# A ring of four weight buffers for both expert matmuls of a hybrid encoder block, with VectorE's work spread over a written-out loop

## What is computed

```python
q = (xt @ wq).reshape(T, PEER_HEADS, 2, PEER_HALF)
v1, i1 = lax.top_k(s1, PEER_TOPK)              # s1, s2: q against two sets of 128 keys
v2, i2 = lax.top_k(s2, PEER_TOPK)
best, flat = lax.top_k(cand, PEER_TOPK)        # cand: the 16 x 16 sums of v1 and v2
experts = e1 * N_KEYS + e2
gates = jax.nn.softmax(best, axis=-1)
a = jnp.einsum("td,thkd->thk", xb, u[eb])      # eb: 8 heads x 16 experts of a token
act = gb * jax.nn.gelu(a)
y = jnp.einsum("thk,thkd->td", act, v[eb])
```

## Time and profile before

| what | value |
|---|---|
| device time, median of 3 runs | 3211.02 us (3209.46 to 3213.96) |
| the profiled execution, first to last instruction | 3210.7 us |
| PE busy | 3014.2 us (94%) |
| DVE busy | 2610.3 us (81%) |
| ACT busy | 1091.2 us (34%) |
| POOL busy | 825.0 us (26%) |
| first to last v job's start | 2181.9 to 3205.9 us |
| first to last gelu of a u job | 1088.5 to 2181.5 us |

### The profile page before, as it was taken

One profiled execution on the slowest core, in us unless ns is written; L12 is line 12 of the kernel. 1 busy time (PEld: TensorE's weight loads), 2 busy tenths in 40 slices (PEclk: granted clock), 3 DMA queues, 4 the chain that ended last, 5 costly groups with the idle time before them and its releaser, 6 DMA issues.

```text
span 3210.7 us, 44193 instructions
## 1 busy us (share of the span) xinstructions
PE 3014.2 (94%) x17373; PEld 2771.7 (86%) x17373; DVE 2610.3 (81%) x3085; ACT 1091.2 (34%) x1132; POOL 825.0 (26%) x380
## 2 busy tenths in 40 slices
PE   4899989989899989999999999997899999999999
PEld 2687766557678989999989999987899999999999
DVE  6986868766763599999879999875798898988985
ACT  3322243431122334444323333322333333333331
POOL 4600000000020012333102322332354544444440
PEclk8999989999999999999999999998999999999999
DMA  8621224257644358778648999998899999999994
GB/s 359 262 99 71 72 86 154 103 217 299 256 170 158 142 191 297 295 290 299 250 177 340 356 365 367 367 372 336 342 379 392 391 385 389 383 388 394 384 389 158
DMA packets 182046, 892.83 MB, mean 278 GB/s; under 512 B 15664, under 2 KB 77232, under 8 KB 85808
## 3 DMA queue, kind: packets, MB, share of 16 engines
q1 hardware_dynamic: 111376, 491.29, 40.8%
q0 software_dynamic: 46080, 335.56, 26.6%
q10 hardware_dynamic: 24480, 64.45, 5.1%
HBM read 836.71 MB, written 54.53 MB: 278 GB/s over the span
## 4 chain that ended last, share of the span: by engine, by line
PE 73%; DVE 14%; DMA 6%; ACT 3%; issue 3%; POOL 1%; SPq 0%; DVEq 0%; ACTq 0%; PEldq 0%
PE bank L1592 11%; PE bank L1593 11%; PE bank L1594 11%; PE bank L1951 8%; PE bank L1953 8%; PE bank L1952 8%; PE bank L1925 2%; DVE w_lo L905 2%; DVE ada_w L930 2%; PE bank L1829 2%; PE bank L1830 2%; PE bank L1831 2%; DMA ada_w<-wada 1%; DMA u_row<-u_rows,urow_i 1%; PE bank L1634 1%
## 5 line engine op out<-in xcount | busy, mean ns | idle before, releaser
L1592 PE MATMUL bank<-act_hi,w_hi 128*128 128x352 f32 (+1 forms) x2584 | 886.7, 343 | 42.6 <-DVE w_lo L905 32.0
L1593 PE MATMUL bank<-act_lo,w_hi 128*128 128x352 f32 (+1 forms) x2584 | 879.5, 340 | 0.0
L1594 PE MATMUL bank<-act_hi,w_lo 128*128 128x352 f32 (+1 forms) x2584 | 876.9, 339 | 0.0
L1951 PE MATMUL bank<-wt_hi,w_hi 128*128 128x352 f32 x2048 | 666.2, 325 | 34.0 <-ACT stage L854 14.6
L905 DVE TENSOR_TENSOR w_lo<-w_raw,w_hi 128x2048 fp32r<-128x2048 f32 (+1 forms) x191 | 434.7, 2276 | 282.1 <-ACT w_hi L472 269.1
L1952 PE MATMUL bank<-wt_lo,w_hi 128*128 128x352 f32 x2048 | 662.5, 323 | 0.0
L1953 PE MATMUL bank<-wt_hi,w_lo 128*128 128x352 f32 x2048 | 662.4, 323 | 0.0
L472 ACT ACTIVATE w_hi<-w_raw 128x2048 fp32r<-128x2048 f32 (+1 forms) x199 | 375.6, 1887 | 810.2 <-PE bank L1594 547.5
L1592 PEld LDWEIGHTS bank<-act_hi,w_hi 128*128 128x128 f32 x2584 | 491.7, 190 | 71.3 <-issue 26.9
L1594 PEld LDWEIGHTS bank<-act_hi,w_lo 128*128 128x128 f32 x2584 | 493.4, 191 | 22.3
L1593 PEld LDWEIGHTS bank<-act_lo,w_hi 128*128 128x128 f32 x2584 | 492.3, 191 | 20.8 <-issue 0.2
(11 more groups left out here) (297 smaller groups left out, 3801.0 us busy)
## 6 DMA issues: line engine op xcount, KB each, us to landing
w_raw<-u SPq DMA_DIRECT2D x128, 1024.0 KB, 8.1
w_raw<-v SPq DMA_DIRECT2D x86, 1024.0 KB, 9.3
ada_w<-wada SPq DMA_DIRECT2D x80, 1024.0 KB, 5.8
v_raw<-v SPq DMA_DIRECT2D x42, 1024.0 KB, 9.3
w_raw<-win SPq DMA_DIRECT2D x27, 1024.0 KB, 4.8
gelu_scratch<-gelu_s ACTq DMA_DIRECT2D x128, 176.0 KB, 3.6
gate_scratch<-g_chunk ACTq DMA_DIRECT2D x11, 2048.0 KB, 14.3
wt<-gelu_scratch SPq DMA_DIRECT2D x32, 704.0 KB, 5.5
```

The source lines that it names most:

```text
L1592: pe.matmul(out, wh, hi_t(k), start=(k == 0), stop=False)
L1593: pe.matmul(out, wh, lo_t(k), start=False, stop=False)
L1594: last = pe.matmul(out, wl, hi_t(k), start=False, stop=(k == nk - 1))
L1951: pe.matmul(o, w_hi[s][:, col], th, start=begin is not None and e == 0, stop=False)
```

## The change

One ring of four buffers takes the raw weights of u and v jobs alike. The low half is written over the raw weight it was made of, so raw and low share a buffer, and three buffers hold high halves. The load of job g now waits until PE has finished job g-4, `hi` until PE has finished g-3. The u jobs are written out on all engines, and what DVE does between them is dealt out anew: selections write their results in place, 7 dots in 6 jobs instead of 6 in 6, three jobs for each block of indices instead of four, four more rows of `u` are gathered before the switch. The hot steps run with jobs 74 to 117 instead of 72 to 115. ACT does the gelu of a job before the high half of the job three ahead. The end of a segment no longer waits for PE's own last matmul.

```diff
+XU = 12
+SEL_G, TAB_G, SEL, TAB, HOT = 2, 10, 13, 61, 74
+N_HOTS = TD // 8
...
-        v_raw = [w_raw[J_V % 2], w_raw[1 - J_V % 2], at("v_raw2", 54, [P, CH])]
+        raw = [w_raw[1], w_raw[0], at("raw2", 104, [P, CH]), at("raw3", 96, [P, CH])]
+        low = [at("low0", 72, [P, CH], F32R), at("low1", 64, [P, CH], F32R), w_lo[1], w_lo[0]]
+        hi_side = at("hi_side", 32, [P, KD, T], F32R)[:, :, T - P:T]
+        hi_v = at("hi_v", 54, [P, CH], F32R)
...
+            def load_raw(g):
+
+                if g < 2:
+                    wait_lo(sp, J_U - 2 + g)
+                else:
+                    sp.wait_ge(pe_jobs, J_U + g - 3)
+                sp.dma_start(raw[g % 4][:], u_d[g] if g < NKEY else v_d[v_index(g - NKEY)]).then_inc(raw_loaded[g % 4], 16)
...
+            def hi_raw(g):
+
+                act.wait_ge(raw_loaded[g % 4], 16 * (g // 4 + 1))
+                act.wait_ge(pe_jobs, J_U + (g - 2 if g > 2 else min(g - 1, 0)))
+                act.activation(hi_of(g), in_tiles(raw[g % 4]), ACT.Copy).then_inc(hi_done, 1)
...
-            def gelu_job(u, turn):
-                hi(J_U + 2 + u, turn)
-                act.wait_ge(gelu_stored[u], DMA_LEAD + turn * 16)
-                act.activation(gelu_s[u][:], bank[(J_U + u) % 2][:, 0:TD], ACT.Gelu_apprx_tanh).then_inc(bank_used[(J_U + u) % 2], 1)
...
+            def gelu_job(u):
+
                 b = (J_U + u) % 2
+                act.wait_ge(pe_jobs, J_U + u + 1)
+                act.wait_ge(gelu_stored[u % 2], DMA_LEAD + 16 * (u // 2))
+                act.activation(gelu_s[u % 2][:], bank[b][:, 0:TD], ACT.Gelu_apprx_tanh).then_inc(bank_used[b], 1)
+                act.wait_ge(bank_used[b], LEAD + BU_U0[b] + u // 2 + 1)
+                act.dma_start(gelu_d[:, u:u + 1, :], gelu_s[u % 2][:].unsqueeze(1)).then_inc(gelu_stored[u % 2], 16)
+                hi_raw(u + 3)
...
+            def lo_raw(g):
+
+                dve.wait_ge(hi_done, J_U + g + 1)
+                dve.tensor_tensor(in_tiles(low[g % 4]), in_tiles(raw[g % 4]), hi_of(g).bitcast(F32), ALU.subtract).then_inc(lo_done, 1)
...
-            build_hots(0, 0)
-            with dve.Fori(0, N_HOT - 1) as i:
-                T_.open(i, 2)
-                for u in range(2):
-                    lo(J_U + 74 + u, i)
-                    build_hots(1 - u, i + u)
-                    for m in range(1 + u):
-                        dot(54 + u + m, i, 3)
-                T_.close(N_HOT - 1)
...
+            lo_raw(HOT - 1)
+            build_hots(0)
+            for t in range(N_HOTS):
+                lo_raw(HOT + t)
+                if t < N_HOTS - 1:
+                    build_hots(t + 1)
+                for m in range(1 + t % 2):
+                    dot(n_dot)
+                    n_dot += 1
...
-            for n in range(118, NKEY):
-                lo(J_U + n)
-                for m in range(2):
-                    if n < 122:
-                        dot(120 + 2 * (n - 118) + m)
-                    elif n < 126:
-                        dot_x(2 * (n - 122) + m)
-                if n == 125:
+            for n in range(HOT + N_HOTS, NKEY):
+                lo_raw(n)
+                for m in range(2 if n_dot < P + 8 else 1):
+                    if n_dot < P:
+                        dot(n_dot)
+                    elif n_dot < P + XU:
+                        dot_x(n_dot - P)
+                    n_dot += 1
+                if n == 122:
                     weigh(0)
-            weigh_lo(0)
+                elif n == 124:
+                    weigh_lo(0)
+                elif n == 126:
+                    weigh(1)
...
-            with pe.Fori(0, N_HOT) as i:
-                for u in range(2):
-                    u_job(u, i + 36)
-                    pe.wait_ge(hot_ready[u], i + 1)
...
+            for t in range(N_HOTS):
+                u_job(HOT + t)
+                u = t % 2
+                pe.wait_ge(hot_ready[u], t // 2 + 1)
...
-                        elif e == 1 and end:
+                        elif e == 1 and end and d < 7:
                             last.then_inc(seg_sum, 1)
...
-                elif end:
-                    pe.wait_ge(seg_sum, 8 * end)
-                    pe.sem_inc(pe_jobs, 1)
```

More of the change, by code:

```diff
@@ L23 @@
 N_CH = TD // GC
-N_HOT = TD // 16
 EPS = 1e-6
@@ L443, in _ @@
             pool.wait_ge(h2x_set, 4)
-            for n in range(P + 8):
+            for n in range(P + XU):
                 if n >= 3:
@@ new lines, in keep_hots @@
+            def keep_hots(t):
+                chunk, at_, cb = t // 4, 8 * (t % 4), t // 4 % 2
+                if t % 4 == 0:
+                    act.wait_ge(g_stored[cb], DMA_LEAD + 16 * (chunk // 2))
+                for g in range(2):
+                    act.wait_ge(hot_used[2 * (t % 2) + g], LEAD + t // 2 + 1)
+                    act.activation(g_chunk[cb][:, :, at_ + 4 * g:at_ + 4 * g + 4], bank[2 + g][:].rearrange("p (t i) -> p i t", t=4),
+                                   ACT.Copy).then_inc(g_copied[g], 1)
+                if t % 4 == 3:
+                    for g in range(2):
+                        act.wait_ge(g_copied[g], LEAD + t + 1)
+                    act.dma_start(gate_d[chunk], g_chunk[cb][:]).then_inc(g_stored[cb], 16)
@@ L780, in _, with weigh_hi @@
+            def weigh_hi(n):
+                act.wait_ge(wt_ready, n + 1)
+                act.activation(wt_hi[n % 4][:], wt[:], ACT.Copy).then_inc(wth_ready, 1)
+            gelu_job(0)
+            gelu_job(1)
             act.wait_ge(h2x_ready, 4)
@@ L794, in _ @@
[L794 to L804, removed]
-                            act.activation(g_chunk[cb][:, :, bass.ds(b * 16 + (8 * u + 4 * g), 4)],
-                                           bank[2 + g][:].rearrange("p (t i) -> p i t", t=4),
-                                           ACT.Copy).then_inc(g_copied[g], 1)
-                for g in range(2):
-                    act.wait_ge(g_copied[g], LEAD + c * 8 + 4 * cb + 4)
-                act.dma_start(gate_d[c * 2 + cb], g_chunk[cb][:]).then_inc(g_stored[cb], 16)
@@ L843, in _ @@
-            for u in range(2):
-                gelu_last(u)
+            for u in range(2, NKEY):
+                gelu_job(u)
+                if u == TAB_G - 2:
+                    act.wait_ge(gmax_ready, 1)
+                    act.activation(expd_g[:], shifted_g[:], ACT.Exp).then_inc(gexp_ready, 1)
+                if TAB <= u < TAB + 3 * GB and (u - TAB) % 3 == 0:
+                    act.wait_ge(gmax_ready, 2 + (u - TAB) // 3)
+                    act.activation(expd[:], shifted[:], ACT.Exp).then_inc(gexp_ready, 1)
+                if HOT <= u < HOT + N_HOTS:
+                    keep_hots(u - HOT)
+                if u == 122:
+                    act.wait_ge(dots_done, P)
+                    act.activation(a_g[:], a_g[:], ACT.Gelu_apprx_tanh).then_inc(act_g_ready, 1)
+                if u == 123:
+                    weigh_hi(0)
@@ L1418, in _ @@
             T_.step(dve.tensor_tensor(sel[:], sel[:], ident[:, 3 * XT:4 * XT], ALU.add))
+            lo_raw(TAB + 10)
+            for m in range(2):
+                dot(n_dot)
+                n_dot += 1
+            lo_raw(TAB + 11)
             dve.wait_ge(tabt_ready, 3)
@@ L1901, in _ @@
                     last.then_inc(h2x_ready, 1)
-            with pe.Fori(1, 35) as i:
-                for u in range(2):
-                    u_job(u, i)
-            u_job(0, 35)
+            for u in range(2, TAB + 10):
+                u_job(u)
             pe.wait_ge(tables_ready, 1)
```

298 lines of the change are left out of this document (121 added, 177 removed).

## The result

| | before | after |
|---|---|---|
| device time, median of 4 runs | 3212.49 us (3209.46 to 3215.55) | 3191.15 us (3183.65 to 3194.86) |
| the profiled execution, first to last instruction | 3210.7 us | 3187.1 us |

The ratio is 0.9929, interval 0.9917 to 0.9941: faster by 0.7%. Forecast were 3162, 3130 to 3190: the direction was right, the gain less than half of what the prediction added up, and the median lies 1 us outside the range.

What follows compares the result with a forecast made beforehand. PE bounds the kernel, with at most 87 us to win. 3210.7 - 12.2 (A) - 17.4 (B) + 20 (C) - 28.6 (D) - 6.6 (E) - 4.0 (F) = 3161.9, forecast 3162 us, range 3130 to 3190.

Steps and rivals of the forecast that it cites:

- C: Hot steps: DVE's build, dots and low half 0.9 us late in 21 steps, 20 us lost (13 to 25).
- R1: Rival: the hot steps do not stall, so 3142 us instead of 3162; chance 0.20.
- R3: Rival: short waits in the hot steps lower PE's clock to a mean 0.87, 60 us more, 3222; chance 0.07.
- A and B: u jobs around blocks of indices: A (1140 to 1200 us) gains 12.2 us, B (1575 to 1665) 17.4 us.
- D: The switch from u to v jobs, 2070 to 2300 us: loss 44.1 falls to 15.5, gain 28.6 (14 to 38).
- steps (1) to (3): At the switch, losses left: 6 us by load volume, 1.5 for a low half behind `weigh(1)`, 1 for a gelu.
- E and F: E, each segment end: PE's wait for its last matmul goes, 6.6 us; F, 3120 to 3140 us: gain 4.0.
- Step (4): At the switch: first eviction behind `weigh_hi(2)` and a high half, its unit's load beside `acc_o`'s 4 MB, 3 us left.
- Step (1): At the switch: 23.5 MB asked in jobs 118 to 123 needs 59 us against 46.4 of matmuls; 6 us left.
- step (5): At the switch: PE's clock lowered after the waits, 4 us left.
- R2: Rival: memory is the ceiling; E and F give nothing, the switch takes 7 us more, 3180 us; chance 0.17.
- R4: Rival: the lead is never built up; A, B, F and most of D gain nothing, 3204 us; chance 0.06.

Runs made afterwards that it cites:

- e2: The changed kernel without the 66 gathers of rows 58 to 123, their dots working on whatever the buffers hold: 3170.02 us.
- e8: The kernel of e3 with each high half made one job later, so ACT works one job ahead rather than two: 3158.12 us.
- e10: The kernel of e9 without the 4 MB load into `acc_o`, four ACT copies of a small tile standing in: 3135.88 us.
- e11: The kernel of e9 with the 4 MB load cut into eight 512 KB pieces, one after each high half from v job 2 to 9: 3139.7 us.
- e6: The kernel of e3 with `weigh(3)` done one v job later on DVE and ACT: 3149.38 us.
- e9: The kernel of e6 with `weigh(0)` one u job later (job 122 to 123), and the low parts of units 0 and 1 too: 3144.03 us.
- e4: The changed kernel with PE's wait for its own last matmul at the end of a segment put back: 3194.94 us.
- e3: The changed kernel with the dots of a hot step ahead of the build of the one-hot tables instead of behind it: 3151.69 us.
- e5: The kernel of e3 with the 4 MB load into `acc_o` issued three v jobs later, DVE waiting for it before the first add: 3157.39 us.

## Why the prediction was right in sign and wrong in size

**C, the hot steps: mechanism right, term too small.** Forecast 20 us lost, measured 33.6. The chain that the prediction worked out, 0.9 us late in each of 21 steps, is what e2 shows (19.5; 21 x 0.91 is 19.1, which the prediction rounded up). What failed is that it ended its count at DVE's own work: neither the 20 nor the upper end of 25 has a term for rows that land late or for the clock behind a longer wait. Ten rows landed 16.1 to 17.8 us after they were asked for and were needed after 15.8; with rows PE's waits are 9.7 us longer than without, and the clock took about 4.4: 14.1 more. R1 (no stall) fell. R3 (the half clock) did not come: the clock was 0.99 over 1700 to 2060.

**A and B: right in size.** Gain forecast 29.6, measured 32.8. The working put it to the lead and to the work taken off DVE; e8 shows that the lead carries 4 to 8 of it.

**D, the switch: wrong size.** The forecast left 15.5 us of loss and put the gain at 28.6; it is 13.6. On the u side, from the last hot step to the first v job, the loss against jobs of 7.73 fell from 18.6 to 13.7 us, where steps (1) to (3) left 8.5: a gain of 4.9. On the v side the first ten v jobs, against 7.64 us each, lost 27.8 before and 19.0 after: a gain of 8.7. The rest of the v side's 19.6 is about 7.5 of E and 3.4 of F. Step (4), 3 us for the eviction and `acc_o`, failed. It looked for the wait at the eviction (1.5 there) and missed two in front of it, of 5.8 each: v job 3's weights stand behind the 4 MB (e10 and e11 take this wait away) and a low half behind `weigh(3)` (e6 takes that one away). Step (1), the lateness by volume, has a rival cause now: in the kernel of e6 a 7.0 us wait ended, for 1.3 one job later (e9), by moving one wait of DVE by a job, with no byte less. How the u side's excess of 5.2 over steps (1) to (3) divides between them and the clock of step (5) stays open.

**E and F: right.** Forecast 6.6 and 4.0. The v loop holds 47 matmuls more (7.5 us), 41 of which go again with e4, and 3120 to 3140 has 124 where full pace is 124.5. The prediction read 0.47 us at an end of a segment; with the job behind it 0.55 were lost at each.

**R2, the ceiling of memory, fell.** 391 GB/s over 780 us, at PE busy 780.00. The Trainium skill, HBM Reference, Specifications (TRN2), gives a core's effective share as about 358 GB/s, and about 425 for a core that streams alone; the trace's 391 lies between, so the share is not a lone core's limit here, as the prediction had it. R4 fell with A and B.

**The sum.** 3161.9 forecast and 3187.1 measured, 25.2 apart: C 13.6 and D 15.0 too good, A and B together 3.2 too modest, E and F together 0.3. The bounds of C and D were each too narrow, and both erred to the same side.

## What to carry to other kernels

When a wait is brought closer to what it waits for, price it, and then ask what is queued behind it on its engine, which transfers are timed by that work, and what they will meet: here a chain that is 20 us too long cost 34. Before a deeper buffer is built, try the order: work that needs nothing of the other engine goes in front of the wait (e3: 39 us for three lines moved, more than the whole change gave). At a switch between phases look up, for each in-order wait on a load, how long ago that load was issued and what big transfer was issued just ahead of it; cut the big one into pieces, and put the wait a job later rather than moving the transfer whole (e9 and e11 against e5).

## What the runs showed of the hardware that was not expected

- A 4 MB load issued in one piece by ACT's queue delayed by some 10 us a 1 MB load that SP's queue issued 6 to 8 us later: v job 3's weights took 15.2 to 16.5 us from issue to landing with it ahead (the changed kernel, e3, e6, e9), 4.8 in e5 and 4.7 in e11, where the first of the eight pieces stands ahead.
- The clock followed PE's waits, but not by their length alone. Waits of 1.9, 2.0 and 2.4 us in the hot steps were followed by ten to twelve matmuls 0.29 us apart (clock 0.91 in those 20 us slices, with 116 to 133 matmuls of some 157) and then by 0.16 again. The longest there, 2.8 us, was followed by 0.16 at once, in a slice at 1.00. With the waits all at 0.7 or less (e2) the clock stayed at 1.00, though PE was not busy for 13 of 360 us.
- A wait of PE costs about 0.25 us more than the profile shows as idle: 0.30 shown and 0.55 lost at a segment's end (e4), 0.69 shown and 0.93 lost in a hot step (e2).
- A gather of 128 rows (1 MB) took at most 13.7 us from asking to landing in the hot steps of the kernel before, and 16.1 to 17.8 in ten cases of the changed one, each right behind another gather and some 3 us ahead of a 2 MB store.
